# Two fp32r products of a high and a low part in place of one fp32 product, at five norms of a two-block kernel

## The reference, cut to what matters

```python
def rms_norm(x, g):
    xf = x.astype(jnp.float32)
    y = xf * lax.rsqrt(jnp.mean(xf * xf, axis=-1, keepdims=True) + EPS)
    return (y * g.astype(jnp.float32)).astype(x.dtype)

n = rms_norm(h, attn_norm[i]);  z = n @ w_in[i]                     # norm 0 of the kernel
m = rms_norm(h, mlp_norm[i]);   h = h + square(relu(m @ w_mlp_up[i])) @ w_mlp_down[i]   # norm 1
gate = sigmoid(rms_norm(h, ple_norm[i]) @ w_ple_gate[i] + b)        # norm 2
h = rmsnorm(x, ffn_norm[i]);    x = x + conv_ffn(h, ...)            # norms 4 and 6 (i = 0, 1)
```

## Time and profile before

| what | value |
|---|---|
| median of 3 runs | 1650.19 us (1648.57 to 1650.54) |
| the profiled execution's own time | 1649.77 us |
| its span, first to last instruction | 1648.0 us |
| granted TensorE clock, mean | 0.999 |
| TensorE (PE) busy | 1639.9 us |
| VectorE (DVE) busy | 938.9 us |
| ScalarE (ACT) busy | 615.4 us |
| GpSimd (POOL) busy | 84.5 us |

### The profile page before, as it was taken

How to read it: one execution, slowest core, us unless ns; L and a number is a source line. 1 busy time by engine, 2 the same in 40 slices (tenths; PEclk the granted TensorE clock), 3 DMA queues, 4 the chain that set the end, 5 groups by cost and what they waited for, 6 DMA issues and landing times.

```text
span 1648.0 us, 19096 instructions
## 1 busy us (share of the span) xinstructions
PE 1639.9 (100%) x8084; PEld 1336.8 (81%) x8084; DVE 938.9 (57%) x1384; ACT 615.4 (37%) x828; POOL 84.5 (5%) x80
## 2 busy tenths in 40 slices
PE   9999999999999999999999999999999999999999
PEld 7877878888888888888888888877777888888887
DVE  6797675444343546577466457545655577366353
ACT  5576433332222336433223223455555333122121
POOL 1300000000000000000000000311201100000000
PEclk9999999999999999999999999999999999999999
DMA  5300227444453421222322222322221233222311
GB/s 195 116 26 27 103 77 131 132 87 110 100 119 83 123 103 52 77 103 102 128 77 102 103 83 96 126 77 92 85 76 52 77 103 103 102 102 93 109 60 71
DMA packets 27910, 155.94 MB, mean 95 GB/s; under 512 B 3696, under 2 KB 5120, under 8 KB 11952
## 3 DMA queue, kind: packets, MB, share of 16 engines
q1 hardware_dynamic: 26352, 149.84, 25.4%
q0 software_dynamic: 1328, 4.86, 5.1%
q10 hardware_dynamic: 144, 0.00, 0.0%
HBM read 149.98 MB, written 4.72 MB: 94 GB/s over the span
## 4 chain that ended last, share of the span: by engine, by line
PE 96%; DVE 2%; ACT 1%; POOL 0%; DMA 0%; issue 0%; SPq 0%; DVEq 0%
PE bank L584 26%; PE bank L586 26%; PE bank L585 26%; PE bank L590 3%; PE bank L592 3%; PE bank L591 3%; PE bank L1215 1%; PE bank L1225 1%; PE bank L1241 1%; PE bank L839 1%; PE bank L824 1%; PE bank L1101 0%; PE bank L1203 0%; PE bank L768 0%; PE bank L606 0%; PE bank L864 0%
## 5 line engine op out<-in xcount | busy, mean ns | idle before, releaser
L584 PE MATMUL bank<-AH,WH 128*128 128x512 f32 (+1 forms) x1150 | 451.4, 393 | 1.5 <-DVE gsil L2007 1.4
L586 PE MATMUL bank<-AH,WL 128*128 128x512 f32 (+1 forms) x1150 | 447.8, 389 | 0.0
L585 PE MATMUL bank<-AL,WH 128*128 128x512 f32 (+1 forms) x1150 | 447.6, 389 | 0.0
L1674 DVE TENSOR_TENSOR WL<-RAW,WH 128x2048 fp32r<-128x2048 f32 (+1 forms) x133 | 298.5, 2247 | 189.9 <-ACT WH L1286 189.9
L1286 ACT ACTIVATE WH<-RAW 128x2048 fp32r<-128x2048 f32 (+1 forms) x133 | 248.3, 1871 | 258.9 <-PE bank L586 240.3
L584 PEld LDWEIGHTS bank<-AH,WH 128*128 128x128 f32 (+1 forms) x1150 | 215.5, 187 | 49.9 <-issue 2.6
L586 PEld LDWEIGHTS bank<-AH,WL 128*128 128x128 f32 (+1 forms) x1150 | 215.5, 187 | 46.0
L585 PEld LDWEIGHTS bank<-AL,WH 128*128 128x128 f32 (+1 forms) x1150 | 215.5, 187 | 45.3 <-issue 1.0
L584 PE MATMUL bank<-HH,WH 128*128 128x512 f32 x608 | 239.6, 394 | 0.0
L586 PE MATMUL bank<-HH,WL 128*128 128x512 f32 x608 | 238.4, 392 | 0.0
L585 PE MATMUL bank<-HL,WH 128*128 128x512 f32 x608 | 236.0, 388 | 0.0
(11 more groups left out here) (305 smaller groups left out, 1733.1 us busy)
## 6 DMA issues: line engine op xcount, KB each, us to landing
RAW<-in_W SPq DMA_DIRECT2D x124, 1024.0 KB, 4.8
RAW<-in_W SPq DMA_DIRECT2D x9, 768.0 KB, 4.2
X<-in_XT SPq DMA_DIRECT2D x16, 256.0 KB, 5.3
ev_scratch<-ev POOLq DMA_DIRECT2D x16, 160.0 KB, 7.7
Gb<-ev_scratch SPq DMA_DIRECT2D x16, 128.0 KB, 3.2
out<-X SPq DMA_DIRECT2D x8, 256.0 KB, 2.0
Gb<-ev_scratch SPq DMA_DIRECT2D x16, 112.0 KB, 2.7
RAW<-in_W SPq DMA_DIRECT2D x2, 512.0 KB, 5.2
```

What stands on the lines that cost most here:

```text
L584: e.matmul(o, a, h, start=first, stop=False)
L585: e.matmul(o, a, l, start=False, stop=False)
L586: return e.matmul(o, c, h, start=False, stop=last)
L1674: e.tensor_tensor(k.WL[j][:, 0:n], k.RAW[RAW_OF[u]][:, 0:n], k.WH[j][:, 0:n].bitcast(F), SUB).then_inc(*WLO.mark(u))
```

## The change

`diagonal` takes the tile that it writes. `spread_rows` on DVE copies r4 to rh (rounded to fp32r), takes rl = r4 - rh, and writes two diagonal tiles of fp32r, diagH in dg's place and diagL in sq0's place. `norm_spread` on TensorE makes two fp32r products with fp32r ones (onesr), added up in bank 7, in place of one fp32 product. onesr is filled once by a DVE copy of 128 by 128, behind `mean_square(0)`. The spread of norm 0 moves: it now stands behind the first two chunks (six products) of the first gq tile. The new tiles take 576 bytes of each partition, so that the tiles behind them lie higher. diagH1 and diagL1 are declared and not used. The norms' spreads of the GLA output (`spread_out`, L935) stay as they are.

```diff
@@ memory
+    rb_at = a.at
     k.rb = a.tile("rb", [P, S])
+    sq_at = a.at
     k.sq = [a.tile(f"sq{i}", [P, S]) for i in range(2)]
...
+    k.onesr, k.rh, k.rl = a.tile("onesr", [P, P], R), a.tile("rh", [P, 4], R), a.tile("rl", [P, 4])
     k.m4 = a.tile("m4", [P, 4])
+
+    k.diagH = [a.over(f"diagH{i}", [P, 4, P], at, R) for i, at in enumerate((dg_at, rb_at))]
+    k.diagL = [a.over(f"diagL{i}", [P, 4, P], sq_at + 4 * S * i, R) for i in range(2)]
@@ tensor_program
     def norm_spread(i):
         w.wait_ge(DVE("rdiag", i), *free[7])
-        e.matmul(bank[7][:, :], ones, k.acc, start=True, stop=True).then_inc(*MM.mark("spread", i))
+        e.matmul(bank[7][:, :], k.onesr[:, :], k.diagH[0][:, :, :], start=True, stop=False)
+        e.matmul(bank[7][:, :], k.onesr[:, :], k.diagL[0][:, :, :], start=False, stop=True).then_inc(*MM.mark("spread", i))
         free[7] = [ACT("rb", i)]
...
-    norm_spread(0)
...
     for i in range(2):
         b = next_bank(6)
         w.wait_ge(*free[b])
-        product(u, 8, i, b).then_inc(*in_bank(b, "gq", i))
+        if i == 0:
+            product(u, 8, i, b, ks=range(2))
+            norm_spread(0)
+        product(u, 8, i, b, ks=range(0 if i else 2, 8)).then_inc(*in_bank(b, "gq", i))
@@ vector_program
-    def diagonal(r):
-        return e.tensor_tensor(dg[:, :, :], ident[:, None, :].to_broadcast([P, 4, P]), r[:, :, None].to_broadcast([P, 4, P]), MUL)
+    def diagonal(o, r):
+        return e.tensor_tensor(o[:, :, :], ident[:, None, :].to_broadcast([P, 4, P]),
+                               r[:, :, None].to_broadcast([P, 4, P]), MUL)

     def spread_rows(i):
         w.wait_ge(POOL("r4", i))
-        diagonal(k.r4[:, :]).then_inc(*DVE.mark("rdiag", i))
+        e.tensor_copy(k.rh[:, :], k.r4[:, :]).then_inc(*DVE.mark("rh", i))
+        w.wait_ge(DVE("rh", i))
+        e.tensor_tensor(k.rl[:, :], k.r4[:, :], k.rh[:, :].bitcast(F), SUB).then_inc(*DVE.mark("rl", i))
+        diagonal(k.diagH[0], k.rh[:, :].bitcast(F))
+        w.wait_ge(DVE("rl", i))
+        diagonal(k.diagL[0], k.rl[:, :]).then_inc(*DVE.mark("rdiag", i))
...
     mean_square(0)
     w.wait_ge(arrived(k, "cst"))
+    e.tensor_copy(k.onesr[:, :], cst[:, C_ONE:C_ONE + P])
     spread_rows(0)
```

## The result

The changed kernel takes **1657.0 us** (median of 5 runs, 1656.6 to 1657.06) against 1650.19 (5 runs, 1648.57 to 1650.54). The ratio is 1.0045, interval 1.0034 to 1.0056: 6.8 us slower. The forecast was 1648.7, the range ended at 1650.2. The profiled execution took 1657.0 us, its span is 1655.2 (before 1648.0).

What follows compares the result with a forecast made beforehand. PE bounds the kernel, a queue of products with hardly a gap (96% of the span). Shorter spreads -2.0 us and norm 2's wait +0.5 give -1.5, so 1650.19 becomes 1648.7 us; range 1646.9 to 1650.2.

Steps and rivals of the forecast that it cites:

- Tiles moved by 576 bytes, sq0 written again.: Memory places: nobody waits for sq0 and no row shows a cost for an address, so zero.
- Two fp32r products for one of fp32: PE at five norms: three fp32r products, 0.69 us, in place of 1.10 us; 2.0 us less in all.
- DVE's longer way: DVE ahead of rdiag: four operations, together 1.59 us in place of 0.69, so rdiag comes 0.90 us later.
- Norm 2: Spread at norm 2: the load waits for rdiag, PE stands still for 0.49 us, bounds 0.26 to 0.75.
- Norm 0: Spread at norm 0, moved behind six products: rdiag comes 0.78 us early, no wait.
- Norms 1, 4, 6: Spreads at these norms: rdiag still early (2.3 us at norm 4), no cost; 1.10 us becomes 0.69.
- Queue of DVE behind norm 0: DVE's work behind norm 0 comes 0.98 us later; 2.2 and 1.4 us to spare, cost nothing.
- Rival D: Behind norm 0: DVE's queue loses 2 us more, sums behind gq wait; 1649.3 or so, chance 0.04.
- Sum of the norms: All five norms together: -2.0 + 0.5 = -1.5 us, from -1.75 to -1.25.
- A: PE's low clock at 196 to 200 us goes away: 1.7 us less, 1647.0; chance 0.11.
- B: A second low-clock stretch, at 165 to 200 us or norm 2: 1.7 us each, one gives 1650.4; chance 0.08.
- Rival C: The spread's products run at fp32 pace, 0.87 us each: 4.9 us more, 1655.0; chance 0.03.

Runs made afterwards that it cites:

- e1: The kernel before with 576 unused bytes left free behind r4, where the new tiles would be, norms untouched: 1658.14 us, ratio 1.0051.
- e6: The kernel before with 64 bytes left free behind r4: span 1655.1 us at clock 1.000 (one run).
- e3: The kernel before with 192 bytes left free behind r4: 1643.37 us, ratio 0.996.
- e11: e7 with norm 2's spread, and ACT's read of it, issued one tile of proj later: span 1641.7 us (one run).
- e10: e7 with norm 0's spread back in its old place ahead of gq, with the new products: span 1642.3 us at clock 0.999 (one run).
- e2: The changed kernel with onesr, rh and rl at the top of the partition, all other tiles at their old places: 1647.3 us, ratio 0.9988.
- e7: The changed kernel with 128 more bytes left free, so that HH comes to distance 0 from the weights: 1643.53 us, ratio 0.9965.
- e8: The kernel before with 448 bytes left free behind r4: span 1645.1 us at clock 0.998 (one run).
- e9: The kernel before with 64 bytes free ahead of RAW, so RAW, WH, WL and all behind lie higher, AH stays: 1672.04 us (one run).
- e4: The kernel before with each of the 20 HH and HL tiles 64 bytes further than a stride of 2048: span 1652.4 us (one run).

## Why the prediction was wrong

The step that failed is a single one: "*Tiles moved by 576 bytes, sq0 written again.* ... No row shows a cost for an address: zero." The runs put 8.4 us in its place (e1; e6 the same), 7.8 of them in the HH and HL products, which stand 233.3 ns apart in place of 229.0. With the norm part of -1.5 that makes +6.9 at equal clock (1655.2 against 1648.3), which is what the medians say. No row of before shows an address cost as a wait. But a row shows a hint that was there to be read: HH and HL products of one shape had 394, 392 and 388 ns where AH's had 392, 389 and 389, and their spacing was 229 against 227. A difference between products that differ in nothing but their tiles is a price of the tile. It was in the kernel before with some 4 us (e3). A place that costs something already can cost another amount when it changes, so the term should have had a range and a rival on the slow side.

The other steps, one by one:

- *Two fp32r products for one of fp32*: 3 starts at 0.23 us, as forecast. The 131 ns of the Trainium skill (TensorE: Matmul & The Clock Gate, Back-to-back issue gap) are not seen in any run; no group of products of 512 columns has a mean spacing under 225 ns.
- *DVE's longer way*: 1.57 us, forecast 1.59, with the first two starts 0.21 apart and the diagonals 0.60.
- *Norm 2*: the load comes 0.47 us late (604.93 in place of 604.46), as forecast (0.49), but PE loses 0.35. I took the load's delay for PE's. With PE empty the second load starts 0.11 us after the first (605.04) and the product is not held for 0.23. The value lies inside the bounds (0.26 to 0.75); the loss was over-sized by 0.14, or by 0.11 if e11's 0.38 is taken.
- *Norm 0*: no wait with the move, 0.86 us to spare; 0.45 us without it (e10).
- *Norms 1, 4, 6*: 0.39, 0.40 and 0.39 us saved, forecast 1.10 - 0.69 = 0.41.
- *Queue of DVE behind norm 0*: 2.2 and 1.5 us to spare, forecast 2.2 and 1.4. Rival D did not happen.
- *Sum of the norms*: -1.5 by e2 against before, -1.4 by e7 against e3, both at the same clock; forecast -1.5. Had the tiles stood still, the forecast of 1648.7 would have held: e2's runs at before's clock of 0.999 took 1648.5 to 1648.7.
- *Rivals A and B, the low clock*: both are real, in other runs of other kernels (A in e3, B in e8). In the profile of after the low stretch is there as in the earlier trace rows, a little earlier; in e3 it is gone; in e8 it is twice as long. Windows of the three, in that order (us; PE, PEld, DVE, ACT, POOL busy; granted clock, DMA share, GB/s):

```profile
189.00:196.00 7.00, 7.00 (x66) 6.59 (x65) 2.18 (x4) 2.21 (x4) 0.35 (x1) 0.91 0.10 41
196.00:200.00 4.00, 4.00 (x15) 3.18 (x14) 2.07 (x1) 1.90 (x2) 1.29 (x1) 0.74 0.00 0
```

```profile
196.00:200.00 4.00, 4.00 (x19) 3.28 (x18) 2.39 (x2) 1.57 (x1) 0.96 (x1) 1.00 0.00 0
```

```profile
189.00:196.00 7.00, 7.00 (x66) 6.61 (x65) 2.06 (x4) 1.99 (x4) 0.00 (x0) 0.92 0.15 64
196.00:200.00 4.00, 4.00 (x10) 3.13 (x11) 1.64 (x2) 2.43 (x2) 1.64 (x1) 0.50 0.00 0
200.00:204.00 4.00, 4.00 (x15) 3.19 (x15) 3.41 (x6) 0.00 (x0) 0.00 (x0) 0.79 0.47 188
```

  In after (0.09 x 7 + 0.26 x 4) x 2 = 3.3 us at half speed, 1.7 lost; in e8 (0.08 x 7 + 0.50 x 4 + 0.21 x 4) x 2 = 6.8 us, 3.4 lost. All five runs of after were at clock 0.999, as the profiled run of before was: the clock has no part in the result. It differs from run to run of the same kernel, and so was scatter and not a cause. In the sizes that the prediction gave them neither A nor B could have led to 1657.0.
- *Rival C*, products at the pace of fp32: not seen.

Not settled: why the distance matters. In the traces the load for the next product runs beside the product, and two reads that get in each other's way would fit a dependence on distance alone; but that is argued, no run shows it. e9 moved RAW together with WH and WL, so the writes of DMA, ACT and DVE moved too; that every product of a stretch shows the same pattern, whatever those do at the time, speaks against them, but they were not tried by themselves. Nor was it tried whether the distance counts for tiles of other widths than 512 columns of four bytes, or how a product's neighbours enter (e4).

## What to carry to other kernels

A new tile can have a price even if nobody waits for it: it moves every tile behind it. Where products stream without a gap, keep each tile that streams at a distance of a multiple of 256 bytes per partition from the tiles that are loaded as weights (here 226.7 ns a product against 233.3: 12.0 us of 1650 for the 1824 products of HH and HL, 411.2 to 423.2, and 21.3 for the 3400 of AH and AL), and put small new tiles at the end. Compare spacings, start to start, between groups of one shape: a group that is 1% slower than another tells of this with no wait in sight.

## What was not expected of the hardware

- The pace of an fp32r product depends on the distance of its two tiles: 226.7, 229.0, 233.3 and 233.3 ns at 0, 64, 128 and 192 bytes modulo 256. It repeats: stretches of 192 products of HH and HL in one trace agree within 0.01 us, and within one the spacings run in patterns of three (232, 226, 229 at distance 64) or two (229, 237 at 128).
- The scatter of the runs is not noise. Spans of before lie at 1646.7, 1648.3 or 1650.2 and hardly between. The profiled runs go with it: no time at the lower clock level behind the light stretch near 200 us in e3 (mean clock 1.000), 3.4 us in before (0.999), 6.8 in e8 (0.998). Between runs of the same mean clock, which here agree within 0.8 us, a difference of 1 us in 1650 can be read, where medians over mixed levels stray by 2.
